# Two-layer hybrid trunk on one Trainium2 core: the next expert's first two gate pairs moved between "up" and "down"

## What is computed

```python
xe = h[bidx, top_i]                            # 96 or 64 rows of 1024
a = jnp.einsum('becd,edf->becf', xe, w_gate)   # 1024 x 1408
u = jnp.einsum('becd,edf->becf', xe, w_up)     # 1024 x 1408
y = jnp.einsum('becf,efd->becd', jax.nn.silu(a) * u, w_down) * top_w[..., None]
return jnp.zeros_like(h).at[bidx, top_i].add(y)
```

## Time and profile before

| | us |
|---|---|
| median of the runs | 4424.52 |
| the profiled execution's own time | 4431.7 |
| its span | 4429.9 |
| PE, busy in the span | 3673.1 (83%) |
| DVE, busy | 2318.7 (52%) |
| ACT, busy | 1813.0 (41%) |
| mean share of PE's full clock | 0.806 |
| DMA, mean | 154 GB/s |

### The profile page before, as it was taken

The page is one execution under the profiler, slowest core; times in us unless marked ns, Lnnn a source line. Parts: engine busy times, 40 slices in busy tenths (PEclk is TensorE's granted clock), DMA queues, the critical chain, the costliest instruction groups (busy, mean ns, idle before and its releaser), DMA issues.

```text
span 4429.9 us, 59181 instructions
## 1 busy us (share of the span) xinstructions
PE 3673.1 (83%) x24115; PEld 2632.4 (59%) x24115; DVE 2318.7 (52%) x3029; ACT 1813.0 (41%) x2325; POOL 340.9 (8%) x100
## 2 busy tenths in 40 slices
PE   6999997776849889988888999887767577887777
PEld 1565777775526666666634657687664366666666
DVE  0112325558446777777731203345583577777767
ACT  1112222113126677777621112311232467767766
POOL 0000000000011111111100000000000112121111
PEclk9998557685879999999999995576757788888888
DMA  7210000000147888888863100000002688878775
GB/s 256 75 39 19 0 1 2 2 2 2 39 167 289 307 327 318 307 306 309 303 220 120 53 19 1 1 2 2 2 2 85 239 292 316 317 294 301 297 299 210
DMA packets 180696, 680.12 MB, mean 154 GB/s; under 512 B 15435, under 2 KB 25759, under 8 KB 180383
## 3 DMA queue, kind: packets, MB, share of 16 engines
q1 hardware_dynamic: 166088, 637.81, 37.8%
q0 software_dynamic: 6144, 20.98, 2.0%
q10 hardware_dynamic: 8283, 18.67, 1.1%
HBM read 656.44 MB, written 20.97 MB: 153 GB/s over the span
## 4 chain that ended last, share of the span: by engine, by line
PE 61%; DVE 16%; DMA 9%; issue 7%; ACT 6%; ACTq 1%; SPq 0%; DVEq 0%; POOL 0%; PEldq 0%
PE ps L687 11%; PE ps L1803 11%; PE ps L1775 8%; DMA gu<-in_moe_w_up 7%; PE ps L1261 6%; PE ps L918 4%; PE ps L941 4%; PE ps L1602 3%; DVE down_lo L2010 3%; ACT hi L1865 3%; DVE gu_lo L2010 2%; PE ps L641 2%; DMA arena<-in_w_mod 2%; PE ps L931 2%; PE ps L1810 1%
## 5 line engine op out<-in xcount | busy, mean ns | idle before, releaser
L2010 DVE TENSOR_TENSOR gu_lo<-gu,hi 128x2816 fp32r<-128x2816 f32 x256 | 782.7, 3087 | 354.3 <-ACT hi L1865 354.3
L1865 ACT ACTIVATE hi<-gu 128x2816 fp32r<-128x2816 f32 x256 | 640.4, 2549 | 136.0 <-DMA gu<-in_moe_w_up 127.3
L1775 PE MATMUL ps<-hi,xsplit 128*96 128x512 f32 (+3 forms) x2304 | 576.4, 397 | 99.7 <-ACT hi L1865 88.2
L1775 PEld LDWEIGHTS ps<-hi,xsplit 128*96 128x96 f32 (+1 forms) x2304 | 411.8, 183 | 230.6 <-ACT hi L1865 108.2
L2010 DVE TENSOR_TENSOR down_lo<-down,hi 128x1024 fp32r<-128x1024 f32 (+1 forms) x256 | 417.5, 1654 | 172.5 <-ACT hi L1865 172.5
L687 PE MATMUL ps<-arena 128*128 128x512 f32 (+2 forms) x1536 | 501.7, 488 | 7.1 <-PE ps L687 4.3
L1775 PE MATMUL ps<-gu_lo,xsplit 128*96 128x512 f32 (+3 forms) x1536 | 416.4, 410 | 85.9 <-DVE gu_lo L2010 85.2
L687 PEld LDWEIGHTS ps<-arena 128*128 128x128 f32 x1536 | 290.5, 190 | 217.1 <-issue 191.7
L1775 PEld LDWEIGHTS ps<-gu_lo,xsplit 128*96 128x96 f32 (+1 forms) x1536 | 282.0, 192 | 194.6 <-DVE gu_lo L2010 133.2
L1865 ACT ACTIVATE hi<-down 128x1024 fp32r<-128x1024 f32 (+1 forms) x256 | 343.6, 1373 | 123.4 <-PE ps L1803 123.2
L1261 PE MATMUL ps<-arena 64*64 64x64 f32 (+1 forms) x6080 | 266.1, 234 | 27.0 <-DVE arena L1039 21.5
(11 more groups left out here) (292 smaller groups left out, 4986.6 us busy)
## 6 DMA issues: line engine op xcount, KB each, us to landing
gu<-in_moe_w_gate SPq DMA_DIRECT2D x256, 704.0 KB, 6.1
gu<-in_moe_w_up SPq DMA_DIRECT2D x256, 704.0 KB, 8.0
down<-in_moe_w_down SPq DMA_DIRECT2D x64, 2048.0 KB, 7.9
arena<-in_w_mod SPq DMA_DIRECT2D x24, 2048.0 KB, 7.7
down<-in_moe_w_down SPq DMA_DIRECT2D x32, 1536.0 KB, 9.8
arena<-in_w_in SPq DMA_DIRECT2D x6, 2048.0 KB, 7.6
arena<-in_w_out SPq DMA_DIRECT2D x4, 2048.0 KB, 9.8
arena<-in_w_in SPq DMA_DIRECT2D x4, 1536.0 KB, 7.3
```

The source lines that it names most:

```text
L1775: ins = nc.tensor.matmul(ps[0:lhs.shape[1], 3 * m + b, 0:n], lhsT=lhs, rhs=w[:, c0 + 512 * b:c0 + 512 * b + n], start=(row == 0 and stage ...
L1865: nc.scalar.activation(hi_part(u), whole(u), ACT.Copy).then_inc(hi_a.sem, 1)
L2010: nc.vector.tensor_tensor(lo_part(u), whole(u), hi_part(u).bitcast(F32), ALU.subtract) \
```

## The change

Steps are renamed p. Expert e's body now has p = 0 to 5 (its pairs 2 to 7), then p = 6 and 7 (pairs 0 and 1 of expert e + 1), then down as p = 8 to 15. Expert 0's pairs 0 and 1 run ahead of the loop; the last expert has no p = 6, 7. PE turns h between p = 6 and p = 7. The split x has two buffers, and PE's and ACT's loops do two experts per iteration. PSUM banks are moved so that the next gate can start while the up part is still read. SP loads pairs 2 to 7, the next expert's 0 and 1, then down. POOL gathers for e + 2 ahead of the scatter of e. A one-element Silu stands at the head of ACT's loop.

```diff
+def use(p, is_last=False):
+    return p + LEAD - (2 if is_last and p >= PAIRS else 0)
+def pair(p):
+    return (p + 2) % PAIRS
...
 # SP
+            with sp.Fori(1, NE - 1) as e:
+                for k in range(2, PAIRS):
                     gate_up(e, k)
+                gate_up(e + 1, 0)
+                gate_up(e + 1, 1)
                 for n in range(3):
                     downs(e, n)
-                for k in range(4, 8):
-                    gate_up(e, k)
...
 # PE
+            def gate_up(e, p, par, is_last):
+                k = pair(p)
+                xs = (xsplit2 if folded(layer) else xsplit3)[par if p < 6 else 1 - par]
+                if k == 0:
+                    pe.wait_ge(xe_p.sem, e + xe_p.n(layer, 2 if p == 6 else 1))
+                    if p == 6 and not folded(layer):
+                        pe.wait_ge(h_a.sem, e * 3 + h_a.n(layer, 3))
...
+            def expert(e, par, is_last):
+                if folded(layer) and not is_last:
+                    turn_x(e + 1)
+                for p in range(6):
+                    if p == 2:
+                        pe.wait_ge(ye_v.sem, e * 2 + ye_v.n(layer, 1))
+                        if not folded(layer) and not is_last:
+                            turn_x(e + 1)
+                    if folded(layer) and p == 4:
+                        pe.wait_ge(gate_cp.sem, e * 3 + gate_cp.n(layer, 3))
+                        if not is_last:
+                            pe.wait_ge(xe_w.sem, e * 2 + xe_w.n(layer, 4))
+                        for ft in range(FT):
+                            fold(gate_c, ft)
+                    gate_up(e, p, par, is_last)
+                if not is_last:
+                    gate_up(e, 6, par, is_last)
+                turn_h(e)
+                if not is_last:
+                    gate_up(e, 7, par, is_last)
+                for p in range(PAIRS, USES):
+                    downs(e, p, is_last)
...
 # ACT, layer 1 (folded), then layer 0
+                for p in range(2, 5):
+                    high(e, p, is_last)
                 if folded(layer):
+                    if not is_last:
+                        gathered(e + 1, 1 - par)
...
+                    high(e, 5, is_last)
...
+                    for p in steps(6, 7, is_last):
+                        high(e, p, is_last)
+                    if not is_last:
+                        gathered(e + 1, 1 - par)
+                    for p in steps(7, 10, is_last):
+                        high(e, p, is_last)
...
 # DVE, both layers
+                for p in steps(2, 9, is_last):
+                    low(e, p, is_last)
+                dve.wait_ge(used.sem, e * USES + used.n(layer, use(5) + 1))
```

More of the change, by code:

```diff
@@ L444, in trunk_program @@
         hTl = sem("hTl")
+        gu_free = sem("gu_free")
+        down_free = sem("down_free")
         h_a = sem("h_a")
@@ L1842, in expert @@
-                for u in range(PAIRS, USES):
-                    downs(e, u)
-            turn_x(0)
-            with pe.Fori(0, NE - 1) as e:
-                expert(e, False)
-            expert(NE - 1, True)
+                        fold(up_c, ft)
+                    return
+                for b in range(3):
+                    pe.wait_ge(h_v.sem, e * 3 + h_v.n(layer, b + 1))
+                    for ft in range(4 * b, min(4 * b + 4, FT)):
+                        ins = nc.tensor.transpose(ps[:, 3 + b, (ft % 4) * CAP:(ft % 4 + 1) * CAP],
+                                                  sg[0:CAP, ft * P:(ft + 1) * P], ident[0:CAP, 0:CAP])
+                    ins.then_inc(htm.sem, 1)
@@ L1897, in expert @@
                                              ps[:, 6 + half, 0:(f1 - f0) * CAP_L], ACT.Silu).then_inc(sil_a.sem, 1)
-                    high(e, 8)
-                    high(e, 9)
-                    act.wait_ge(used.sem, e * USES + used.n(layer, PAIRS))
+                    for p in steps(7, 9, is_last):
+                        high(e, p, is_last)
+                    act.wait_ge(used.sem, e * USES + used.n(layer, use(5) + 1))
                     for b in (0, 2):
@@ L1908, in expert @@
                         nc.scalar.activation(hsplit[:, f0:f1, 0, :], h2[:, f0:f1, :], ACT.Copy).then_inc(hs_a.sem, 1)
-                    for u in range(10, USES):
-                        high(e, u)
-                    act.wait_ge(used.sem, e * USES + used.n(layer, USES))
+                    for p in range(10, USES):
+                        high(e, p, is_last)
+                    act.wait_ge(used.sem, e * USES + used.n(layer, use(USES - 1, is_last) + 1))
                     for half in range(2):
@@ L1915, in expert @@
                 else:
-                    act.wait_ge(used.sem, e * USES + used.n(layer, 4))
+                    high(e, 5, is_last)
+                    act.wait_ge(used.sem, e * USES + used.n(layer, use(1) + 1))
                     for b in range(3):
@@ L1940, in act_experts @@
             nc.scalar.activation(affc[:, :, 0:NE], affc[:, :, 0:NE], ACT.Exp).then_inc(aff_a.sem, 1)
+            high(0, -2)
+            high(0, -1)
+            act.wait_ge(x_out.sem, x_out.n(layer, 16))
             high(0, 0)
             high(0, 1)
[L1943 to L1949 removed]
+            gathered(0, 0)
+            with act.Fori(0, NE - 2, 2) as e:
+                nc.scalar.activation(silu_table[:, :], ident[:, 0:1], ACT.Silu)
+                expert(e, 0, False)
+                expert(e + 1, 1, False)
+            expert(NE - 2, 0, False)
+            expert(NE - 1, 1, True)
         def dve_choose(dve, layer):
```

221 lines of the change are left out of this document (100 added, 121 removed).

## The result

| | before | after |
|---|---|---|
| median of the runs shown with the result, us | 4423.7 | 4298.43 |
| those runs, us | 4419.36 to 4425.82 | 4287.3 to 4388.68 |
| span of the profiled execution, us | 4429.9 | 4386.9 |

What follows compares the result with a forecast made beforehand. No engine fills an expert's period; PE comes nearest, with waits and half clock besides. Layer 0 -13, layer 1 -56, prologue +2 make -67 us against 4431.7: 4364.7, with the median 7.2 lower 4358 us; range 4312 to 4440.

Steps and rivals of the forecast that it cites:

- Layer 1: Layer 1's experts: period falls from 59.0 to 55.3 us, -3.7 x 15 = -56 us.
- the named waits: Layer 1: 3.61 us after down, up folds waiting for DVE's copy, half clock at p = 7, down landing at 24.0.
- the row's 413: DMA rate in GB/s taken from the trace for the loads; at 358 the forecast would be 4385 us.
- Layer 0: Layer 0's experts: period falls from 58.5 to 57.6 us, -0.9 x 15 = -13 us; PE waits 5.3 us before p = 6.
- pair 7 lands at 5.9: Layer 0: pair 7's load lands 5.9 us after the end of p = 1 frees its buffer.
- lands at 10.7; I add 1.0: Layer 0: the next expert's pair 0, freed at 4.8, lands at 10.7, plus 1.0 us for the last expert's scatter.
- rival 1: Late loads: landings above 5.85 us cost each period 0.8 (layer 0) and 1.0 us (layer 1); 4465 us, chance 0.18.
- turning point of 8.4: Rival 1's landing time, in us, at which the change's gain turns into a loss.
- The sum: Whole kernel: -13 - 56 + 2 = -67 us, the +2 for the prologue.
- nothing else is changed: Outside both expert stages, 1.9 of the 4.4 ms, no stage was taken to change.
- Rival 3: PE restarts at full clock after split waits in the experts: periods 55.9 and 53.5 us, 4305 us in all; chance 0.11.

Runs made afterwards that it cites:

- d_down: The changed kernel with SP's order alone undone, down's loads between pairs 3 and 4 again: 4447.48, 4452.05, 4454.22 and 4558.57 us.
- no_scat: The changed kernel with the scatter-add of the expert outputs left out: 4242.56 us, one execution.
- w_before: The kernel before the change with 16 unread matmuls ahead of the scores in both attentions: 4351.17, 4348.99, 4456.2 and 4453.77 us.
- f_before: The kernel before the change with 6, 9 and 6 unread matmuls in the three idle stretches at the start of both attentions: 4346.65 to 4364.82 us.
- s_before: The kernel before the change with 32 unread matmuls in layer 0's attention alone: one execution 4357.37 us, five 4453.52 to 4461.84.
- w_after: The changed kernel with 16 unread matmuls ahead of the scores in both attentions: 4334.51, 4319.38, 4321.98 and 4429.07 us.
- f_after: The changed kernel with 6, 9 and 6 unread matmuls in the three idle stretches at the start of both attentions: 4315.05 to 4333.96 us.
- x_first: The changed kernel with ACT's `gathered(e + 1)` ahead of the hi of p = 4 in layer 0: 4279.65, 4299.97, 4400.94 and 4404.98 us.
- f_xdve: x_dve with 6, 9 and 6 unread matmuls in the three idle stretches at the start of both attentions: 4237.72 to 4256.18 us.
- g_xdve: x_dve with 1, 2 and 1 unread matmuls in the idle stretches of layer 1's attention alone: 4214.06 to 4226.94 us, median 4219.74.
- x_dve: x_first with what PE's turn waits for moved ahead of the last hi and lo, both layers: 4226.11, 4215.31, 4313.5 and 4322.52 us.
- a_same: The changed kernel, unchanged, executed again: 4294.09, 4392.68, 4298.74 and 4390.73 us.
- h_256: x_dve with 1, 2, 1 matmuls starting both attentions and one of 256 columns in each short unit of layer 0's: median 4110.84 us.

## Why the prediction was right or wrong

**Layer 1: right.** 55.3 us forecast, 54.7 measured; -56 us forecast, -59 measured, through the named waits; pair 6 landed in 5.9 us, as forecast. A window there, where pairs and down's first part load behind one another:

```profile
3700.00:3708.00 8.00, 8.00 (x30) 6.74 (x31) 8.00 (x3) 4.64 (x5) 4.85 (x2) 0.76 1.02 377
```

The 377 GB/s are above the 358 that the Trainium skill (DMA: Bandwidth & Descriptors, section Bandwidth) gives per core, which the prediction weighed, and below the row's 413; down's hi waited 3.36 us for it where 2.2 were forecast (24.0 against 21.8). d_down shows that the loads' order carries it.

**Layer 0: right chain, one term too small.** From the end of p = 1 (1473.08 in the profile) p = 6 was to begin at 21.7 and began at 24.2. The term is the two landings, "pair 7 lands at 5.9" and pair 0's "lands at 10.7; I add 1.0": measured are 7.8 for pair 7, and pair 0's hi at 14.2 instead of 11.7. These 2.5 us are the whole miss of that start. I had taken the landing of an empty queue and 1.0 us for the scatter. Without any scatter (no_scat, counted from 1470.81) pair 0's hi comes at 12.5 and p = 6 at 22.5: so 0.8 us of the miss are there without it, and 1.7 come with it. What follows gives 1.3 us back: p = 6 did run at half clock and took 6.3 us instead of 5.9, but the transposes waited for nothing instead of 0.8, and p = 7 ran at full clock, 3.9 us instead of 4.8. The period is 58.8 instead of 57.6, and the stage became 7.6 us longer instead of 13 shorter. That is rival 1's mechanism, in layer 0 alone: the landings are 7.8 and 9.6 us beside its turning point of 8.4, but layer 1's was 5.9.

**The sum: -67 forecast, -51 in the experts' stages of the two first traces, 26 to 41 in the time with the levels kept apart.** A part of the difference is in layer 0's experts: their stage takes 960.6 us in the trace of before, but 953.7 in w_before, 954.1 in f_before and 954.0 in s_before, which don't touch it. Beside those the change costs it 10 to 14 us (w_after 964.2, f_after 968.0). Layer 1's stage gives back 58.5 us from f_before to f_after, 43.7 from w_before to w_after. The rest lies in stages that aren't changed: f_after is 4.4 us later than f_before at the first gather and 10.0 us longer between the experts' stages (6.6 and 9.9 for w_after). Of the eight traces of the changed loop without a cover in layer 0, seven have the first gather at 1311.7 to 1315.5 us, against 1301.88 in before; but x_first has it at 1303.86. What sets these stages stays open.

**What failed: "nothing else is changed".** The sum went by the experts alone. Two thirds or more of the 125 us (all but 26 to 41) come from layer 1's attention, which the sum put at nothing: its granted clock was 1.00 in 11 of 16 executions of the changed kernel, by their times, and in 4 of 48 before. Its level isn't set by its own instructions alone. The trace of before gave a hint that I didn't read: its attention stages are at half clock with PE busy throughout, and in the page's clock slices they are the lowest. Rival 3 ("The clock stays up", 4305 us) is near the measured 4298 only by number. It spoke of restarts within the experts, and those stayed: p = 6 still ran at half clock.

**The cause of the levels** is shown as far as this: PE idles three times, 3.1 us together, as the attention begins; with those stretches covered 24 of 24 executions are on the lower level (f_before, f_after, f_xdve, g_xdve), with one of the three covered 5 of 8 (w_before, w_after); and layer 0 follows once its short waits are covered too (8 of 8). The Trainium skill (TensorE: Matmul & The Clock Gate, section HAM oscillation — how this bites in real kernels) describes the clock falling at waits between bursts of matmuls, in its example DMA waits of some 3 to 5 us. The traces agree that idle time drops the clock, but here stretches of 0.84 and 1.41 us did it, and the clock then stayed at 0.50 while PE was busy for the rest of the stage.

Open stays why the changed kernel passes the uncovered stretches at full clock in 11 of 16 executions and the one before in 4 of 48. A later start alone didn't do it (s_before, 1 of 6). d_down, with the changed loop and no gain from it, was lower in 3 of 4, so it isn't the shorter time either. Counted together, the kernels with the changed loop and layer 1's stretches uncovered (after, x_first, d_down, x_dve, no_scat) were lower in 19 of 29. I have no run that tells more.

## What to carry to other kernels

Before summing a change, look at the granted clock of every stage, the unchanged ones too. A stage with PE busy throughout at half clock can be worth more than a reordering: here 3.1 us of idle time at its start decided 97 us, where the reordering gave 26 to 41, and covering it cost nothing that shows (g_xdve). When executions of one kernel fall on two levels, compare traces of either level stage by stage before explaining a ratio. And when a loop is reordered, take landings from rows in which the same transfers compete, and look for the second chain that ends close behind the first.

## What the runs showed that I had not expected

- A clock that fell at idle stretches of 0.84 and 1.41 us stayed at 0.50 for the rest of a stage in which PE was 100% busy (from 2668 us on in after), where the same instructions held 1.00 in a_same.
- In layer 0's attention, idle stretches of only 0.54 and 0.53 us within units of ten matmuls stood where the clock fell (f_before); with 256 columns of work in each unit they were gone and it held (h_256).
- In layer 1 the scatter's row on POOL grew from 7.03 us to 10.03, and the split of x then waited 6.9 us for it to land; no row of PE there names POOL as what it waited for.
- Pair 7 takes 7.6 us to land in layer 0 even with the scatter left out (no_scat), where an empty queue gave 5.85.
